# Query weights of a retrieval layer: one of four chunks loaded from another point of the program into other buffers

## What is computed

```
q   = h2 @ w_q                       # 256 tokens x 8 heads x 2 halves x 128
sc  = q . sub_keys                   # 128 scores for each half
top 16 of each half -> 256 pair sums -> top 16 pairs = expert ids; g = softmax of their scores
a   = h2 . u_tab[id];  w = g * gelu(a);  y = sum over 8 x 16 experts of w * v_tab[id]
out = x + gate2 * y
```

## Time and profile before

| | |
|---|---|
| median of 3 runs | 914.94 us (914.37 to 916.85) |
| profiled execution, its own time | 915.68 us |
| its span, first to last instruction | 913.9 us |
| mean granted TensorE clock | 0.972 |
| busy: TensorE / VectorE / ScalarE / GpSimd | 86% / 67% / 38% / 31% |
| read from HBM | 335.11 MB |

### The profile page before, as it was taken

One profiled execution on the slowest core, in us unless ns is written; L12 is line 12 of the kernel. 1 busy time (PEld: TensorE's weight loads), 2 busy tenths in 40 slices (PEclk: granted clock), 3 DMA queues, 4 the chain that ended last, 5 costly groups with the idle time before them and its releaser, 6 DMA issues.

```text
span 913.9 us, 8437 instructions
## 1 busy us (share of the span) xinstructions
PE 782.4 (86%) x2526; PEld 419.4 (46%) x2526; DVE 613.2 (67%) x1420; ACT 345.7 (38%) x1025; POOL 284.7 (31%) x279
## 2 busy tenths in 40 slices
PE   4999999899998999999999878797787777777776
PEld 2377877567544665656563323332332222232222
DVE  6788799833569686957759787768754444455544
ACT  3458678771234243333423332322322222222222
POOL 4000000000134344463437543353353343433310
PEclk9999999999999999999999898899899999999999
DMA  9967444665299999999999999999999999999995
GB/s 374 410 266 287 179 189 189 273 248 236 104 423 420 412 406 421 421 422 421 421 420 422 422 420 422 420 423 421 422 421 423 420 423 420 422 421 423 420 422 212
DMA packets 43236, 336.70 MB, mean 368 GB/s; under 512 B 4788, under 2 KB 4916, under 8 KB 6584
## 3 DMA queue, kind: packets, MB, share of 16 engines
q0 software_dynamic: 37152, 268.45, 70.8%
q1 hardware_dynamic: 6024, 67.72, 18.7%
q10 hardware_dynamic: 16, 0.00, 0.0%
HBM read 335.11 MB, written 1.05 MB: 368 GB/s over the span
## 4 chain that ended last, share of the span: by engine, by line
PE 43%; DMA 41%; DVE 8%; ACT 4%; issue 2%; another core or an unknown queue 1%; POOL 0%; SPq 0%; DVEq 0%; ACTq 0%
DMA ring<-in_peer_uv,eid 19%; PE ps_y L1593 17%; DMA rows<-in_peer_uv,eid 7%; DMA spare<-in_peer_uv,eid 4%; PE bank L1563 4%; DMA extra<-in_peer_uv,eid 4%; DMA v_sb<-in_peer_uv,eid 4%; PE bank L1528 3%; PE bank L1403 2%; PE bank L1405 2%; PE bank L1404 2%; DMA gates<-in_peer_uv,eid 2%; DVE ring L993 2%; PE bank L1543 2%
## 5 line engine op out<-in xcount | busy, mean ns | idle before, releaser
L1593 PE MATMUL ps_y<-ring,diag 128*128 128x512 f32 x464 | 221.5, 624 | 53.7 <-ACT diag L1278 52.8
L993 DVE CUSTOM_DVE_ANT_0 ring<-ring,gates 128x1024 f32<-128x1024 f32 x116 | 140.1, 1225 | 89.3 <-DMA ring<-in_peer_uv,eid 87.6
L565 POOL DMA_INDIRECT ring<-in_peer_uv,eid x116 | 127.9, 1102 | 177.8 <-PE ps_y L1593 126.3
L1266 ACT ACTIVATE mask<-mask 128x2 f32<-128x2 f32 (+1 forms) x130 | 26.4, 203 | 384.8 <-DVE mask L993 379.8
L1593 PEld LDWEIGHTS ps_y<-ring,diag 128*128 128x128 f32 x464 | 88.3, 198 | 179.6 <-issue 92.6
L565 POOL DMA_INDIRECT v_sb<-in_peer_uv,eid x18 | 18.7, 1039 | 256.3 <-DVE eid L899 232.1
L1278 ACT ACTIVATE diag<-ident,mask 128x128 f32<-128x128 f32 x256 | 87.0, 386 | 0.1
L1593 PE MATMUL ps_y<-rows,diag 128*128 128x512 f32 x132 | 63.0, 617 | 12.0 <-ACT diag L1278 9.8
L1271 ACT ACTIVATE mask<-g_sb,mask 128x1 f32<-128x1 f32 x256 | 61.7, 287 | 4.3
L629 DVE TENSOR_TENSOR w_lo<-ring,w_hi 128x512 fp32r<-128x512 f32 x76 | 50.7, 685 | 10.9 <-PE bank L1405 9.4
L993 DVE CUSTOM_DVE_ANT_0 rows<-rows,gates 128x1024 f32<-128x1024 f32 x33 | 40.1, 1226 | 24.3 <-DMA rows<-in_peer_uv,eid 23.6
(11 more groups left out here) (222 smaller groups left out, 1321.3 us busy)
## 6 DMA issues: line engine op xcount, KB each, us to landing
ring<-in_ada_t SPq DMA_DIRECT2D x11, 2048.0 KB, 10.7
ring<-in_in_t SPq DMA_DIRECT2D x10, 2048.0 KB, 10.5
ring<-in_up_t SPq DMA_DIRECT2D x2, 2048.0 KB, 10.1
ring<-in_out_t SPq DMA_DIRECT2D x2, 2048.0 KB, 15.3
kz<-in_peer_t SPq DMA_DIRECT2D x2, 2048.0 KB, 17.7
ring<-in_peer_t SPq DMA_DIRECT2D x2, 2048.0 KB, 11.6
x_sb<-in_x SPq DMA_DIRECT2D x2, 1024.0 KB, 12.5
ring<-in_ada_t SPq DMA_DIRECT2D x2, 1024.0 KB, 22.3
```

What stands on the lines that cost most here:

```text
L565: pool.indirect_dma_start(uv_row(n), None, peer_uv, bass.IndirectOffsetOnAxis(ap=eid[:, n:n + 1], axis=0)).then_inc(s_uv[name], 16)
L993: dve.tensor_tensor_reduce(u_row(n), u_row(n), h2[:, n // P, :], 1.0, 0.0, ALU.mult, ALU.add, adot[:, at:at + 1]).then_inc(s_dot, 1)
L1266: act.activation(gel[:, some], adot[:, at:at + count], ACT.Gelu_apprx_tanh).then_inc(s_gelu, 1)
L1593: ins = pe.matmul(ps_y[:, cut], diag[:, n % ND, :], v_row(n)[:, cut], start=first, stop=last)
```

## The change

Chunk 1 of the query weights is loaded in two DMAs of four blocks each, into V and into `spare`, as soon as the last product of the attention is done. Ring slot 2 (R2a, R2b) takes their part among the buffers of the first rows, and V and `spare` join at rows 52 and 53. So that slot 2 is free sooner, the `up` products of tile 1 are computed in the order (0,0), (1,0), (0,1), (1,1) of column half and group. The squares of the second norm go to `diag` in place of `spare`. The 48 pieces of the late modulation sums are spread over all 19 steps, and three of the additions come at later steps. The last four pairs, not two, go row by row.

```diff
-ADA_LATE = {3: 6, 6: 7, 8: 8, 11: 9, 14: 10}
+ADA_LATE = {3: 6, 6: 7, 10: 8, 14: 9, 16: 10}
-ADA_STEP = 3
+ADA_STEP = (3, 3, 3, 3, 2, 2, 2, 2, 2, 2, 2, 2, 3, 3, 3, 3, 3, 3, 2)
-ALONE = 2
+ALONE = 4
-BUFFERS = [("V", 0), ("E", 0), ("Y", 0), ("G", 0), ("R0a", 0), ("R0b", 0), ("R1a", 0), ("R1b", 0), ("S", 10),
-           ("W", 11), ("X", 12), ("R2a", 52), ("R2b", 53), ("R3a", 76), ("R3b", 77), ("Ka", 88), ("Kb", 89)]
+BUFFERS = [("E", 0), ("R2a", 0), ("R2b", 0), ("Y", 0), ("G", 0), ("R0a", 0), ("R0b", 0), ("R1a", 0),
+           ("R1b", 0), ("W", 11), ("X", 12), ("V", 52), ("S", 53), ("R3a", 76), ("R3b", 77), ("Ka", 88), ("Kb", 89)]
@@ psum_plan
-    items += [("up", 1, 0, 1), ("up", 1, 1, 0), ("up", 1, 1, 1)]
+    items += [("up", 1, 1, 0), ("up", 1, 0, 1), ("up", 1, 1, 1)]
@@ block_kernel
-        peer_place = [K_chunk, ring[:, 2, :, :], ring[:, 3, :, :], K_chunk]
+        def blocks_of(place):
+            return place.rearrange("p (k n) -> p k n", n=512)
+
+        peer_runs = [[K_chunk], [blocks_of(places["V"]), blocks_of(spare[:])],
+                     [ring[:, 3, :, :]], [K_chunk]]
...
+        def peer_block(m, k):
+            return next(run[:, k - first, :] for run, first in zip(peer_runs[m], peer_from[m]) if k < first + run.shape[1])
@@ await_first_use
-            if name == "V":
-                await_item(eng, ("y", 1, 1, 3))
+            if name in "VS":
+                await_item(eng, ("qp", 1, 3))
-            elif name == "S":
-                eng.wait_ge(s_sq4, 4 + 2)
...
-                await_item(eng, {"0": ("o", 1, 0), "1": ("o", 1, 1), "2": ("qp", 1, 3), "3": ("qp", 1, 5)}[name[1]])
+                await_item(eng, {"0": ("o", 1, 0), "1": ("o", 1, 1), "2": ("up", 1, 1, 0), "3": ("qp", 1, 5)}[name[1]])
@@ SyncE
+            def peer_run(m, r):
+                first, last = peer_from[m][r:r + 2]
+                sp.dma_start(peer_runs[m][r], peer_t[m, :, first:last, :]).then_inc(s_peer[m], 16)
...
-            sp.dma_start(peer_place[0], peer_t[0]).then_inc(s_peer[0], 16)
-            await_item(sp, ("up", 1, 1, 0))
-            sp.dma_start(peer_place[1], peer_t[1]).then_inc(s_peer[1], 16)
+            peer_run(0, 0)
+            await_item(sp, ("y", 1, 1, HEAD_PAIRS - 1))
+            for r in range(2):
+                peer_run(1, r)
             await_item(sp, ("up", 1, 1, 1))
...
@@ VectorE, between
-                first = ADA_LATE_FIRST * KD + ADA_STEP * u
-                partials(first, min(first + ADA_STEP, ADA * KD))
+                first = ADA_LATE_FIRST * KD + sum(ADA_STEP[:u])
+                partials(first, first + ADA_STEP[u])
@@ VectorE, order of the products
-            up(1, 0, 1)
-            for g in range(2):
-                up(1, 1, g)
+            up(1, 1, 0)
+            for c_ in range(2):
+                up(1, c_, 1)
@@ ScalarE, squares
+                    act.wait_ge(s_sq4, 4 + n)
-                act.activation(spare[:, cut], x_sb[:, t, cut], ACT.Square,
+                squared = diag[:, 4:8, :] if t else diag[:, 2 * n:2 * n + 2, :]
+                act.activation(squared.rearrange("p a n -> p (a n)"), x_sb[:, t, cut], ACT.Square,
                                accum_out=sq4[:, n:n + 1]).then_inc(s_sq4, 1)
@@ TensorE
-                pe.wait_ge(s_peer[m // 2], 16)
-                w = peer_place[m // 2]
+                pe.wait_ge(s_peer[m // 2], 16 * len(peer_runs[m // 2]))
...
-            up(1, 0, 1, last=1)
+            up(1, 1, 0, last=1)
             turn_h2(0)
             queries(0, 0)
-            up(1, 0, 1, first=1)
-            for g in range(2):
-                up(1, 1, g)
+            up(1, 1, 0, first=1)
+            for c_ in range(2):
+                up(1, c_, 1)
```

More of the change, by code:

```diff
@@ L183, in block_kernel @@
     assert sum(GATE_STEP) == NGATE * KD and len(GATE_STEP) == ALL_STEPS
+    assert sum(ADA_STEP) == (ADA - ADA_LATE_FIRST) * KD and len(ADA_STEP) == ALL_STEPS
     assert TILES == 2 and KD == 8 and GW == 512 and NG * TOPK == ROWS
@@ L324, in block_kernel @@
         halves = peer_uv.rearrange("r (a d) -> (r a) d", d=D)
-        peer_place = [K_chunk, ring[:, 2, :, :], ring[:, 3, :, :], K_chunk]
+        def blocks_of(place):
+            return place.rearrange("p (k n) -> p k n", n=512)
+        peer_runs = [[K_chunk], [blocks_of(places["V"]), blocks_of(spare[:])],
+                     [ring[:, 3, :, :]], [K_chunk]]
+        peer_from = [[sum(run.shape[1] for run in runs[:r]) for r in range(len(runs) + 1)] for runs in peer_runs]
+        def peer_block(m, k):
+            return next(run[:, k - first, :] for run, first in zip(peer_runs[m], peer_from[m]) if k < first + run.shape[1])
         s_small = sem("small_loaded")
@@ L500, in _ @@
             sp.dma_start(x_sb[:], x[0].rearrange("(t p) d -> p t d", p=P)).then_inc(s_x, 16)
-            sp.dma_start(peer_place[0], peer_t[0]).then_inc(s_peer[0], 16)
-            await_item(sp, ("up", 1, 1, 0))
-            sp.dma_start(peer_place[1], peer_t[1]).then_inc(s_peer[1], 16)
+            peer_run(0, 0)
+            await_item(sp, ("y", 1, 1, HEAD_PAIRS - 1))
+            for r in range(2):
+                peer_run(1, r)
             await_item(sp, ("up", 1, 1, 1))
-            sp.dma_start(peer_place[2], peer_t[2]).then_inc(s_peer[2], 16)
+            peer_run(2, 0)
             await_item(sp, ("qp", 1, 1))
-            sp.dma_start(peer_place[3], peer_t[3]).then_inc(s_peer[3], 16)
+            peer_run(3, 0)
             for t in range(TILES):
@@ L1562, in queries @@
                             await_read(pe, ("h2T", t, k // 4))
-                        ins = pe.matmul(b[:, j * P:(j + 1) * P], w[:, k, at:at + P], tT[:, t, k, :],
+                        ins = pe.matmul(b[:, j * P:(j + 1) * P], peer_block(m // 2, k)[:, at:at + P], tT[:, t, k, :],
                                         start=(k == 0), stop=(k == KD - 1))
```

## The result

The changed kernel took 906.86 us (median of 4 runs, 905.79 to 907.84) against 915.27 us before in the same runs: ratio 0.9906, 95% interval 0.9888 to 0.9924, so 8.4 us less. A second sample, beside the last experiments, gave 905.79 us against 915.77 (0.9898, 0.9881 to 0.9915). The forecast was 907.4, 7.5 us less.

A forecast was written before the change was run, and what follows sets the result against it. Compute was taken to bound the kernel up to the first gather, DMA bytes at 421 GB/s after it. Savings of 4.7 (chunk), 2.5 (sums) and 0.35 (single rows) sum to 7.5 us: 907.4 us from 914.94, range 904.2 to 911.5.

The forecast's parts named there:

- the spread sums: Attention: fewer VectorE pieces in steps 4 to 11 cut TensorE's waits, 2.5 us won, bounds 0 and 4.2.
- 0.3 us of added loss: Saturated stage near row 25: engines briefly run dry, taking 0.3 us off the chunk's 4.98; bounds -1.4 and +4.6.
- The two regimes: Up to the first gather at 243.3 us compute sets the time; after it every byte counts at 421 GB/s.
- Are the rows asked for early enough?: Behind the first gather: rows must be requested about 5 us earlier too; tightest at row 25, 0.4 us of cover.
- Its sign of being wrong: Around row 25's issue: under 380 GB/s for 10 us would show the 0.3 us of added loss wrong.
- rival (d): Stretch 305 to 320 us: dry engines hold TensorE at 1.2 GHz for 22 us, 11 us late, 918.4; chance 0.04.
- The compute chain: Behind the first gather: VectorE's landing waits (4.92 us) and TensorE's idle (4.63) go, so buffer releases come 4.6 us earlier.
- The cost side: Attention's end: eight pieces, about 6.2 us of VectorE, move behind the last score and fit, ending near 197.0.
- The single rows: Kernel's end: with single rows the last three adds start 0.4 us earlier; value 0.35 us, bounds 0 and 0.5.
- (a): Attention gains nothing because TensorE's work sets it; time 909.9 us, chance 0.17.
- (b): Behind the first gather: rows asked for as late as before, engines run dry by 4.6 us; 911.7 us, chance 0.13.
- (c): Whole kernel: nothing measurable, (a) and (b) at once; 914.2 us, chance 0.06.

The follow-up runs named there:

- experiment 1: Changed kernel with query chunk 1 issued only after product up(1,0,1), about 1 us after the first gather: 910.67 us, ratio 0.9957.
- experiment 6: Changed kernel with the last two pairs, not four, going row by row: 905.77 us, ratio 0.9902.
- experiment 11: The changed kernel run again unchanged for a second sample and trace: 905.79 us, ratio 0.9898.
- experiment 3: Kernel before with only the new spread of the modulation sums and the new steps of the additions: 911.21 us, ratio 0.9965.
- experiment 8: Changed kernel with the first two query products of tile 1 two pairs later (9 and 12, not 7 and 10): 906.88 us, ratio 0.9917.
- experiment 2: Changed kernel with the late modulation sums as before, three pieces a step in steps 0 to 15: 910.03 us, ratio 0.9950.
- experiment 5: Changed kernel loading query chunk 2 a second time behind the first gather, 2.1 MB more: 911.14 us, ratio 0.9960.
- experiment 9: Changed kernel with half of query chunk 2 also loaded in the idle stretch, into E, and R3a serving first rows instead: 905.22 us, ratio 0.9887.
- experiment 4: Changed kernel loading query chunk 1 a second time in the idle stretch before the first gather, 2.1 MB more: 906.02 us, ratio 0.9905.
- experiment 7: Changed kernel with more modulation sums at the end, four pieces in each of steps 16 to 18, chunk 10 added at step 17: 907.25 us, ratio 0.9918.
- experiment 10: Changed kernel with the up products of tile 1 in the order before, freeing slot 2 one product later: 906.11 us, ratio 0.9901.

## Why the prediction was right

The time came out inside the range, and the two main mechanisms as forecast. One term, the spread sums, was sized too small. What failed is the reading of the dip in the rates, and with it the 0.3 us of added loss.

**The two regimes** and the price of a byte held. Chunk 1 was priced at 4.98 us; undone alone it is 4.9 us in the medians and 5.2 in the stage, doubled elsewhere in the saturated stage 5.1, doubled in the idle stretch 0. The Trainium skill, "DMA: Bandwidth & Descriptors", section "Anatomy of one DMA", fits about 2 us fixed beside the bytes for a DMA issued by GpSimd; for the chunk, which SyncE issues, the prediction made 6.8 us of it. In a full queue that is not borne out: in experiment 1 the chunk stood behind the first gather as two DMAs and was still worth its bytes at 421 GB/s. The limit of about 358 GB/s for a core, which the Trainium skill has in "DMA: Bandwidth & Descriptors", section "Specifications", gives 5.9 us for the chunk, and that was too much as well.

**Are the rows asked for early enough?** The forecast took 0.3 us of added loss at row 25, from a cover of 0.4 us and from the dip of 1.4 us between 316 and 328 in the trace before. The step that failed is that it took the issue time of row 25 in that one trace, and so the cover, as the kernel's own. Its sign of being wrong came too, less than 380 GB/s for 10 us in the trace of the changed kernel:

```profile
298.50:308.50 10.00, 10.00 (x48) 6.42 (x47) 9.69 (x39) 2.81 (x11) 3.62 (x4) 1.00 0.98 374
```

The traces show where the dip comes from. Before row 8's add TensorE waits for ScalarE. In the first trace of the changed kernel that wait is 2.44 us and the add behind it takes 3.45 us (285.11, shown above). In experiment 6, whose kernel differs at its last pairs only, the wait is 2.66 us and the add takes 1.99:

```profile
284.67 1.99 PE L1606 MATMUL ps_y<-ring,diag 128*128 128x512 f32 x4 [2.66 <-ACT diag L1292]
```

The granted clock (third column from the right) from 284.5 to 290.5 us is 0.72, a mix of 2.4 and 1.2 GHz, in the changed kernel's first trace and 1.00 in experiment 6:

```profile
284.50:290.50 6.00, 5.39 (x10) 2.36 (x11) 4.09 (x8) 2.12 (x9) 4.39 (x3) 0.72 1.01 419
```

```profile
284.50:290.50 6.00, 5.83 (x29) 3.92 (x30) 3.66 (x8) 1.68 (x7) 4.89 (x4) 1.00 1.01 422
```

From there on the adds in the first of these traces, and the gathers that wait for them, are about 1.5 us later against the first gather. Row 25's gather goes out 68.2 us after the first, and in experiment 6 66.7 us:

```profile
305.56 0.94 POOL L577 DMA_INDIRECT yT<-in_peer_uv,eid  x1 [4.35 <-PE ps_y L1606]
```

In experiment 11, the changed kernel again, it is 65.6 us. So the schedule of the gathers isn't the same in the two traces of one kernel. The trace before has the same slow add (3.68 us), which the prediction used in its rival (d) alone: its row 25 is asked for 72.3 us after the first gather, and in experiment 3, with the same gathers, 70.6.

The table has the prediction's own count for eight of the 13 traces: cover is the time by which the engines still have work, at 2.49 us a row and 4.98 us a chunk from the end of the first issue, when row 25 has been issued. The last column is the lowest rate in six stretches of 6 us, 54 to 90 us behind the first gather.

| trace | wait before row 8's add, its length | cover at row 25 | lowest rate |
|---|---|---|---|
| before | 2.64, 3.68 | 0.3 | 366 |
| changed kernel, first | 2.44, 3.45 | -0.8 | 355 |
| experiment 8 | 2.41, 3.50 | -0.8 | 356 |
| experiment 2 | 2.60, 1.99 | 0.7 | 406 |
| experiment 6 | 2.66, 1.99 | 0.7 | 412 |
| experiment 11 (changed kernel again) | 1.56, 1.98 | 1.8 | 419 |
| experiment 3 | 2.66, 1.98 | 2.1 | 419 |
| experiment 5 | 2.66, 1.98 | 4.4 | 416 |

The three traces in which row 8's add ran slowly are the three with the least cover, and the only ones of 13 with the dip there. The five traces not in the table have rates of 411 and more; four have 1.7 to 2.1 us of cover, and experiment 9 has 0.8 with the 1.7 us added that its engines had lost earlier. Experiment 5 is the check on the other side: its row 25 is asked for 68.0 us after the first gather, as late as in the first trace of the changed kernel, but one chunk more is queued, and nothing is lost. So the dip is a lack of rows, as the prediction held, but one that comes with an add at a lower clock and not with the kernel. These are comparisons between executions; no run changed the clock of that one add. That the engines' busy share stays at 0.95 to 0.99 in the changed kernel's dip is no objection: in the shortage of experiment 9 it is 0.97 and 0.98 at 373 and 352 GB/s.

What it does to the size of the term: the rates lack 1.4 us in the trace before and 2.1 us in the first trace after, 0.7 more where 0.3 was forecast, and the stage of this pair is 4.7 us shorter. Without the dip on either side it is 670.4 - 665.1 = 5.3 us (experiments 3 and 2), which is the chunk and the tail, 4.98 + 0.25, with no loss. All six traces with the gathers as changed or nearly so and without the dip (experiments 2, 4, 6, 7, 10 and 11) have stages of 665.0 to 665.6 us. That the pair came so close to 4.7 + 0.35 is in part luck: both of its traces have a slow add and a dip, so most of what they cost cancels. The same count found the shortage of experiment 9, 0.9 us at row 7 by the count and 1.7 in the rates.

**The compute chain** moved as told. The waits on landings fell from 4.92 to 0.79 us, row 25's gather from 315.61 to 307.69, of which 3.77 lie before the first gather: 4.15 us against 4.6 forecast. Between the traces with a full clock it is 3.9 us (experiments 3 and 2) and 5.0 (3 and 11).

**The spread sums** were mis-sized: 2.5 us forecast, 3.0 between the traces, 4.0 and 4.2 in medians (experiments 3 and 2). TensorE's waits on ScalarE fell from 3.6 to 2.2 us only:

```profile
PE bank L1516 <- ACT score L1212: 2.2, 3, 1.2
```

The term took TensorE's waits as all that can go. But its busy time in that stretch fell too, with the same matmuls:

```profile
117.77:197.87 80.10, 75.65 (x327) 55.76 (x326) 68.42 (x134) 61.37 (x179) 0.00 (x0) 1.00 0.54 213
```

```profile
117.00:194.10 77.10, 74.45 (x328) 55.98 (x327) 68.38 (x134) 61.47 (x179) 0.00 (x0) 1.00 0.58 225
```

75.65 to 74.45 us is 1.2, and idle fell by 4.45 - 2.65 = 1.8, together 3.0. The profile only models the ends of matmuls, so part of a wait may stand as busy; no run tests that. VectorE's wait for w_ada, 1.9 us before and 2.8 in experiment 2, is gone with the spread. Those 0.9 us are the whole difference between the 90.0 and 91.0 us of the two traces with the old sums. So the spread is worth 3.0 to 3.9 us in the traces, and the 4.0 and 4.2 of the medians hold some of what executions differ by. The cost side fitted: the eight late pieces end 0.9 us before they are wanted.

**The single rows** gave 0.25 us, not 0.35. **Rivals**: (a), no gain in the attention, falls with experiments 2 and 3; (b), rows as late as before, with experiment 1. (c) falls with them. (d), the clock, is wrong in its size, but part of its mechanism is seen. It asked for a TensorE that stops and goes with no cover in the queue, and priced 22 us at 1.2 GHz at 11 us. What the traces show is one slow add and 1.5 us of delay, in experiment 8 two more slow adds at 304.73 and 307.21 us, and in that execution a stage of 907.4 - 239.52 = 667.9 us, 2.3 to 2.9 more than without the dip.

## What to carry to other kernels

Where one stretch of a kernel is bound by its DMA engines and another leaves them idle, a load is worth its bytes when it is moved from the one to the other (here to within 0.3 us), and the place is found by asking which buffers died early. Trade places so that the number of buffers for the saturated stage stays the same, and count the work that is asked for against the engines' rate at each late release. That count also says when the next such move stops paying, as for the half chunk here, of whose 2.5 us the medians show 0.6 and the stage 0.8. Take the issue times for it from more than one execution: a single add at a lower clock moved them by 1.5 us here, more than the 0.4 us of cover that was counted.

## What the runs showed of the hardware

TensorE's granted clock fell after some idle stretches and not after others of the same length. Before row 8's add it waited 2.41 to 2.66 us in eight traces. In three of them (before, the first of the changed kernel, experiment 8) the add took 3.45 to 3.68 us, in five (experiments 1, 2, 3, 5, 6) 1.98 or 1.99. In the five traces in which it waited 1.56 to 1.74 us the clock stayed full. What decides between the two outcomes at the same idle is open.

When the queue of gathers runs short, the rate falls and the busy share of the engines hardly does: 355 to 397 GB/s at shares of 0.95 to 0.99 in the first trace of the changed kernel, and 352 at 0.98 in experiment 9. The loss is also larger than the shortage by the count: 2.1 us in the rates against 0.3 at row 21 and 0.8 at row 25 in the first, 1.7 against 0.9 in the second. Not all of it is in the time. In the first trace of the changed kernel the stage is 0.3 to 0.9 us longer than in the traces without the dip; where the rest is made up is not shown. How much of the spread of experiment 8's single times (905.83, 905.84, 906.57, 907.18, 909.18, 909.67) comes from it is not shown either, since one of them was profiled.
